# Seven block products in place of eight in 14 of the 44 weight pairs of a gated MLP's down product

## What is computed

```python
h = rms_norm(x, ln2[l])
u = h @ w_ffn_in[l]                        # 2048 -> 2 x 5632
a, b = jnp.split(u, 2, axis=-1)
a = causal_depthwise_conv(a, conv_w[l], conv_b[l])
x = x + (jax.nn.gelu(a, approximate=False) * b) @ w_ffn_out[l]   # 5632 -> 2048
return rms_norm(x, ln_f)
```

## Time and profile before

| | us |
|---|---|
| median of 3 runs | 1126.16 |
| lowest and highest | 1125.9, 1127.29 |
| the profiled execution's own time | 1127.33 |
| its span in the trace | 1125.5 |

### The profile page before, as it was taken

One profiled execution on the slowest core, in us unless ns is written; L12 is line 12 of the kernel. 1 busy time (PEld: TensorE's weight loads), 2 busy tenths in 40 slices (PEclk: granted clock), 3 DMA queues, 4 the chain that ended last, 5 costly groups with the idle time before them and its releaser, 6 DMA issues.

```text
span 1125.5 us, 16771 instructions
## 1 busy us (share of the span) xinstructions
PE 1105.9 (98%) x5746; PEld 936.6 (83%) x5746; DVE 693.5 (62%) x994; ACT 565.3 (50%) x800; POOL 75.2 (7%) x86
## 2 busy tenths in 40 slices
PE   7999999999999999999999999999999999999996
PEld 6888888877888888888888888888888788888885
DVE  4656666666655575665656656657566655575555
ACT  5545555555545454544544545445445444455443
POOL 2000111111100000101101101001011000000001
PEclk8999999999999999999999999999999999999999
DMA  9766555554566666666666666666665555556641
GB/s 338 246 188 174 155 165 149 162 155 150 161 190 177 182 187 188 188 187 186 188 190 187 189 190 189 188 187 186 186 187 189 196 191 193 195 186 200 197 133 75
DMA packets 146241, 206.80 MB, mean 184 GB/s; under 512 B 7540, under 2 KB 75538, under 8 KB 145953
## 3 DMA queue, kind: packets, MB, share of 16 engines
q1 hardware_dynamic: 145632, 204.67, 60.3%
q0 software_dynamic: 544, 1.72, 0.4%
q10 hardware_dynamic: 32, 0.01, 0.0%
HBM read 204.17 MB, written 2.10 MB: 183 GB/s over the span
## 4 chain that ended last, share of the span: by engine, by line
PE 97%; DVE 1%; DMA 1%; ACT 0%; SPq 0%; issue 0%; DVEq 0%; ACTq 0%
PE acc L634 14%; PE acc L414 13%; PE acc L416 13%; PE acc L415 13%; PE acc L640 7%; PE bank_s L634 7%; PE bank_tr L634 7%; PE bank_tr L640 4%; PE bank_s L640 4%; PE bank_s L416 2%; PE bank_s L414 2%; PE bank_s L415 2%; PE bank_tr L416 2%; PE bank_tr L414 2%; PE bank_tr L415 2%; DMA raw<-in_w_in 1%
## 5 line engine op out<-in xcount | busy, mean ns | idle before, releaser
L979 DVE TENSOR_TENSOR w_lo<-raw,w_hi 128x1024 fp32r<-128x1024 f32 x380 | 465.8, 1226 | 399.3 <-ACT w_hi L728 397.3
L728 ACT ACTIVATE w_hi<-raw 128x1024 fp32r<-128x1024 f32 x380 | 403.0, 1061 | 542.6 <-PE acc L416 168.0
L634 PE MATMUL acc<-h_both,w_hi 128*128 128x512 f32 x704 | 220.3, 394 | 0.0
L640 PE MATMUL acc<-h_both,w_lo 128*128 128x256 f32 x704 | 140.6, 282 | 0.0
L414 PE MATMUL acc<-w_hi,h_both 128*128 128x512 f32 (+1 forms) x352 | 139.4, 396 | 0.9 <-DVE h_both L986 0.9
L416 PE MATMUL acc<-w_hi,h_both 128*128 128x512 f32 (+1 forms) x352 | 134.6, 382 | 0.0
L415 PE MATMUL acc<-w_lo,h_both 128*128 128x512 f32 (+1 forms) x352 | 134.4, 382 | 0.0
L634 PEld LDWEIGHTS acc<-h_both,w_hi 128*128 128x128 f32 x704 | 121.1, 190 | 15.1
L640 PEld LDWEIGHTS acc<-h_both,w_lo 128*128 128x128 f32 x704 | 121.0, 190 | 13.7
L634 PE MATMUL bank_s<-h_both,w_hi 128*128 128x512 f32 x352 | 109.0, 391 | 0.0
L634 PE MATMUL bank_tr<-h_both,w_hi 128*128 128x512 f32 x352 | 109.0, 390 | 0.0
(11 more groups left out here) (168 smaller groups left out, 1340.1 us busy)
## 6 DMA issues: line engine op xcount, KB each, us to landing
raw<-in_w_ffn_in SPq DMA_DIRECT2D x176, 512.0 KB, 3.6
raw<-in_w_ffn_out SPq DMA_DIRECT2D x88, 512.0 KB, 4.7
raw<-in_w_in SPq DMA_DIRECT2D x128, 256.0 KB, 3.1
raw<-in_w_out SPq DMA_DIRECT2D x32, 512.0 KB, 4.0
raw<-in_w_in SPq DMA_DIRECT2D x20, 512.0 KB, 8.7
x_res<-in_x SPq DMA_DIRECT2D x4, 512.0 KB, 10.3
decay<-table_decay POOLq DMA_DIRECT2D x1, 1024.0 KB, 9.8
lnf_row<-in_ln_f SPq DMA_DIRECT2D x1, 1024.0 KB, 6.7
```

Source lines behind the costliest of these rows:

```text
L634: mm(out, w_hi[:, slot, q * COLS + ft * P:q * COLS + (ft + 1) * P], h_both[:, 2 * k + q, :, :].rearrange("p a n -> p (a n)"), start=k == 0 ...
L640: ins = mm(out, w_lo[:, slot, q * COLS + ft * P:q * COLS + (ft + 1) * P], h_hi[:, 2 * k + q, :], start=False, stop=k == 7 and q == 1, skip ...
L728: run(w_hi[:, n % SPLIT, :], raw[:, n % RAW, :], ACT.Copy).then_inc(hi_ready, 1)
L979: tt(w_lo[:, n % SPLIT, :], raw[:, n % RAW, :], w_hi[:, n % SPLIT, :].bitcast(F32), ALU.subtract).then_inc(lo_ready, 1)
```

## The change

**Seven products.** In 7 of the 22 pairs of each sweep (pairs 2, 5, 7, 10, 12, 15 and 17) the eight block products of a pair become seven, by Strassen's scheme in its form with few sums. Three of the seven take sums of weight blocks (`t_sum`, split to `t_hi` and `t_lo`), four take sums of activation blocks (`g_sums`). DVE makes four sums of 128x512 per such pair (`weight_sums`), one of them in place in the raw tile, so that ACT's rounding of the pair waits for the second sum. The results go to the sweep's own banks and to the four banks of the other sweep; `others_out` adds the latter to `x_res` with six DVE operations, once in a sweep, after a copy by ACT. `g_sums` is made once, in the last up group, by eight DVE operations.

**Pairs.** Weights are split two tiles at a time: one ACT operation and one DVE operation of 2048 columns, in a ring of 3 pairs instead of 4 tiles. There is one `t_sum`, one `t_hi` and one `t_lo`: `t_hi` of a pair waits until TensorE has finished the seven-product pair before it.

**First pairs.** `g_round` and `g_rest` of pairs 0 and 1 move into the last up group. The loops of the down product are written out; the load of `lnf_row` and four `times_gain` move later in the second sweep, the squares of the first sweep to after pair 24's split.

The diff, cut to what is spoken of:

```diff
-G_RING = 8
+PAIR_RING = 3
+DOWN_PAIRS = FFT // 2
+LAST_PAIR = 2 * DOWN_PAIRS - 1
+S_FIRST, S_STEP, S_COUNTS = (2, 5), 5, (4, 3)
+S_SLOT = {first + S_STEP * i: sum(S_COUNTS[:w]) + i
+          for w, (first, count) in enumerate(zip(S_FIRST, S_COUNTS)) for i in range(count)}
+S_PAIRS = sorted(S_SLOT)
+S_SUMS = 4 * len(S_COUNTS)
+X_ADDS = 6
+X_OUT_AT = 20
+GAIN_AT = 18
...
+                if m == 2 * (DOWN_PAIRS + 14) + 1:
+                    sp.wait_ge(g_lo_ready, DOWN_PAIRS + 12)
+                    sp.dma_start(lnf_row[:], ln_f.partition_broadcast(P)).then_inc(lnf_landed, 16)
...
+            def eight_products(r, banks, first=False, last=False):
+                pe.wait_ge(g_lo_ready, r + 1)
+                for half in range(2):
+                    pe.wait_ge(lo_ready, DOWN_TILE + 2 * r + (half + 1 if r < 2 else 2))
+                    for t in range(TOK):
+                        for c in range(2):
+                            ins = down_part(r, half, t, c, banks, first and half == 0, last and half == 1)
+                    ins.then_inc(tile_used, 1)
+            def seven_products(r, banks, others, first, last):
+                hi_g, lo_g, hi_b, lo_b = part_hi(r), part_lo(r), pair_hi(r), pair_lo(r)
+                left, right = slice(0, COLS), slice(COLS, 2 * COLS)
+                def product(out, block, rhs_hi, rhs_lo, starts, stops):
+                    return three_pass(out, hi_g[:, block, :], lo_g[:, block, :], rhs_hi, rhs_lo, starts, stops)
+                pe.wait_ge(g_lo_ready, r + 1)
+                pe.wait_ge(lo_ready, DOWN_TILE + 2 * r + 2)
+                product(others[0][:, 0, :], 0, hi_b[:, 0, left], lo_b[:, 0, left], first, last)
+                product(banks[0][:, 0, :], 2, hi_b[:, 1, left], lo_b[:, 1, left], False, False)
+                product(banks[1][:, 0, :], 7, hi_b[:, 1, right], lo_b[:, 1, right], False, False)
+                product(others[0][:, 1, :], 4, hi_b[:, 0, right], lo_b[:, 0, right], first, last)
+                pe.wait_ge(t_lo_ready, sevens_before(r) + 1)
+                product(others[1][:, 1, :], 6, t_hi[:, 0, :], t_lo[:, 0, :], first, last)
+                product(others[1][:, 0, :], 5, t_hi[:, 1, :], t_lo[:, 1, :], first, last)
+                product(banks[0][:, 1, :], 3, t_hi[:, 2, :], t_lo[:, 2, :], False, False).then_inc(tile_used, 2)
+            def down_pair(r, banks, others):
+                p = r % DOWN_PAIRS
+                if is_seven(r):
+                    seven_products(r, banks, others, p == S_PAIRS[0], p == S_PAIRS[-1])
+                else:
+                    eight_products(r, banks, p == 0, p == DOWN_PAIRS - 1)
...
+            for r in range(DOWN_PAIRS):
+                if r == S_PAIRS[0]:
+                    pe.wait_ge(b_sum_ready, GROUPS * 2)
+                down_pair(r, a_banks, b_banks)
+            pe.wait_ge(x_added, X_ADDS)
+            for r in range(DOWN_PAIRS, LAST_PAIR - 1):
+                if r == DOWN_PAIRS + S_PAIRS[0]:
+                    pe.wait_ge(ffn_added, 2 * TOK)
+                down_pair(r, b_banks, a_banks)
...
-                    pe.wait_ge(lo_ready, DOWN_TILE + m + 1)
+                    pe.wait_ge(lo_ready, DOWN_TILE + 2 * (m // 2) + 2)
                     pe.wait_ge(g_lo_ready, m // 2 + 1)
-                ins = down_part(0, c, (DOWN_TILE + m) % SPLIT, m % G_RING, b_banks, False, m == 87)
+                ins = down_part(m // 2, m % 2, 0, c, b_banks, False, m == 87)
...
+            def g_round(r):
+                if r >= PAIR_RING:
+                    act.wait_ge(tile_used, DOWN_TILE + 2 * (r - PAIR_RING + 1))
+                ins = run(part_hi(r)[:, 0:4, :], g_pair(r), ACT.Copy)
+                if is_seven(r):
+                    act.wait_ge(g_sums_ready, S_SUMS)
+                    ins = run(part_hi(r)[:, 4:8, :], g_sums[:, S_SLOT[r % DOWN_PAIRS]], ACT.Copy)
+                ins.then_inc(g_hi_ready, 1)
+            def hi_pair(r):
+                for n in (DOWN_TILE + 2 * r, DOWN_TILE + 2 * r + 1):
+                    act.wait_ge(raw_landed[n % RAW], landed_value(n))
+                act.wait_ge(tile_used, DOWN_TILE + 2 * max(0, r - PAIR_RING + 1))
+                k = sevens_before(r)
+                if is_seven(r):
+                    act.wait_ge(t_sum_ready, 4 * k + 2)
+                run(pair_hi(r), pair_raw(r), ACT.Copy).then_inc(hi_ready, 2)
+                if is_seven(r):
+                    if k:
+                        before = max(p for p in range(r) if is_seven(p))
+                        act.wait_ge(tile_used, DOWN_TILE + 2 * (before + 1))
+                    act.wait_ge(t_sum_ready, 4 * k + 4)
+                    run(t_hi[:], t_sum[:], ACT.Copy).then_inc(t_hi_ready, 1)
...
+                    if last and k in (10, 11):
+                        g_round(k - 10)
...
-            up_group(GROUPS - 1, FFN_TILE + GROUP_TILES * (GROUPS - 1), 0)
-            for m in (0, 2):
-                g_round(m // 2, m, m)
+            up_group(GROUPS - 1, FFN_TILE + GROUP_TILES * (GROUPS - 1), 0, True)
             b_copies(GROUPS - 1, DOWN_TILE)
...
-            def down_step(m, turn=0, first_kt=0):
-                if m % 2 == 0:
-                    g_round(turn * 4 + (m // 2 + 2), turn * 8 + first_kt, m + 4)
-                hi(DOWN_TILE + m + SPLIT, turn, 8, 16)
...
+            for r in range(2, LAST_PAIR + 1):
+                g_round(r)
+                hi_pair(r)
+                if r % DOWN_PAIRS == X_OUT_AT:
+                    others = (b_banks, a_banks)[r // DOWN_PAIRS]
+                    act.wait_ge(tile_used, DOWN_TILE + 2 * (r - X_OUT_AT + S_PAIRS[-1] + 1))
+                    run(u_sum[:], others[0][:, 0, :], ACT.Copy).then_inc(u_ready, 1)
+                if r == DOWN_PAIRS + 2:
                     for t in range(2 * TOK):
                         last_square_sum(t // TOK, t % TOK, t)
...
+            def g_rest(r):
+                dve.wait_ge(g_hi_ready, r + 1)
+                ins = tt(part_lo(r)[:, 0:4, :], g_pair(r), part_hi(r)[:, 0:4, :].bitcast(F32), ALU.subtract)
+                if is_seven(r):
+                    ins = tt(part_lo(r)[:, 4:8, :], g_sums[:, S_SLOT[r % DOWN_PAIRS]],
+                             part_hi(r)[:, 4:8, :].bitcast(F32), ALU.subtract)
+                ins.then_inc(g_lo_ready, 1)
+            def token_sums(w, k):
...
+                out, in0, in1, op = ((s1, g21, g22, ALU.add), (s3, g11, g21, ALU.subtract),
+                                     (s2, s1, g11, ALU.subtract), (s4, g12, s2, ALU.subtract))[k]
+                tt(out, in0, in1, op).then_inc(g_sums_ready, 1)
...
+                    if last and 3 <= k < 7:
+                        for w in range(len(S_COUNTS)):
+                            token_sums(w, k - 3)
+                    if last and k in (12, 13):
+                        g_rest(k - 12)
...
+            def weight_sums(r):
+                k = sevens_before(r)
+                both = pair_raw(r)
+                b11, b12 = both[:, 0, 0:COLS], both[:, 0, COLS:2 * COLS]
+                b21, b22 = both[:, 1, 0:COLS], both[:, 1, COLS:2 * COLS]
+                for n in (DOWN_TILE + 2 * r, DOWN_TILE + 2 * r + 1):
+                    dve.wait_ge(raw_landed[n % RAW], landed_value(n))
+                if k:
+                    dve.wait_ge(t_lo_ready, k)
+                tt(t_sum[:, 0, :], b22, b12, ALU.subtract).then_inc(t_sum_ready, 1)
+                tt(b12, b12, b11, ALU.subtract).then_inc(t_sum_ready, 1)
+                dve.wait_ge(t_sum_ready, 4 * k + 2)
+                tt(t_sum[:, 1, :], b22, b12, ALU.subtract).then_inc(t_sum_ready, 1)
+                dve.wait_ge(t_sum_ready, 4 * k + 3)
+                tt(t_sum[:, 2, :], b21, t_sum[:, 1, :], ALU.subtract).then_inc(t_sum_ready, 1)
+            def lo_pair(r):
+                dve.wait_ge(hi_ready, DOWN_TILE + 2 * r + 2)
+                tt(pair_lo(r), pair_raw(r), pair_hi(r).bitcast(F32), ALU.subtract).then_inc(lo_ready, 2)
+                if is_seven(r):
+                    dve.wait_ge(t_hi_ready, sevens_before(r) + 1)
+                    tt(t_lo[:], t_sum[:], t_hi[:].bitcast(F32), ALU.subtract).then_inc(t_lo_ready, 1)
...
+            def others_out(sweep):
+                others = (b_banks, a_banks)[sweep]
+                x_0, x_1, x_2, x_3 = others[0][:, 0, :], others[0][:, 1, :], others[1][:, 0, :], others[1][:, 1, :]
+                c0, c1 = (slice((2 * sweep + c) * COLS, (2 * sweep + c + 1) * COLS) for c in range(2))
+                y11, y21, y_2 = x_res[:, 0, c0], x_res[:, 1, c0], x_res[:, :, c1]
+                y2_ = x_res[:, 1, 2 * sweep * COLS:2 * (sweep + 1) * COLS].rearrange("p (c n) -> p c n", c=2)
+                done = sweep * X_ADDS
...
+                dve.wait_ge(tile_used, DOWN_TILE + 2 * (sweep * DOWN_PAIRS + S_PAIRS[-1] + 1))
+                dve.wait_ge(u_ready, sweep + 1)
+                tt(u_sum[:], u_sum[:], x_2, ALU.add).then_inc(x_added, 1)
+                tt(y11, y11, x_0, ALU.add).then_inc(x_added, 1)
```

(25 more changed lines are left out.)

170 lines of the change are left out of this document (70 added, 100 removed).

## The result

The changed kernel takes **1114.51 us** (median of 4 runs, 1114.27 to 1115.29) against 1126.55 (4 runs, 1125.9 to 1127.29) for the kernel before: a ratio of 0.9896, 95% interval 0.988 to 0.9912. The forecast was 1115.8 us, with a range of 1112.5 to 1121.8. The profiled execution of the changed kernel took 1114.47 us, that of before 1127.3.

A forecast was written before the change was run, and what follows sets the result against it. The prediction took TensorE, busy for 98% of the span, to bound the kernel. Its terms -9.5 - 5.0 + 4.1 = -10.4 us, against the median of 1126.2, gave 1115.8 us, with a range of 1112.5 to 1121.8.

The forecast's parts named there:

- Fewer products: Down product: 14 pairs have 21 matmuls for 24, so 42 matmuls at 0.227 us fall away, -9.5 us.
- First pairs: Passage from up to down product: early rounding removes TensorE's 3.3 us wait and 1.7 us of lower clock, -5.0 us.
- VectorE's new load: Down product: VectorE needs 24.7 us per five pairs against TensorE's 25.8, so it keeps up with 4% to spare.
- Waits anew: TensorE waits 1.3 us at pair 2, 0.7 at pair 6, 1.5 at pair 43, plus 0.6 for hand-overs: +4.1 us.
- Costed at nothing: Splitting two tiles in one operation, the `lnf_row` load and what follows the last matmul: no added time.
- The clock drops at the new waits: Rival: three clock drops cost 5.1 us, 1120.9 us; chance 0.17 together with VectorE operations 5% dearer.
- VectorE becomes the bound: Rival: VectorE idles during roundings, losing 2.8 us in each of about six five-pair stretches, 16.8 us: 1132.6 us; chance 0.07.
- The start is late: Rival: a split of the first pairs waits behind the last up tiles, losing the 5.0 us: 1120.8 us; chance 0.05.
- the saving is not there: Rival: extra hand-overs take 0.68 us in each of 14 pairs and the start's gain goes: 1126 us; chance 0.03.
- VectorE is never late: Rival: leads hide the three new waits of TensorE: 1111.7 us, up to 1114; chance 0.08.

The follow-up runs named there:

- e1_eight_products: The changed kernel with eight products in all 44 pairs, without the sums and `others_out`, early rounding kept: 1121.73 us, ratio 0.9959 to the kernel before.
- e7_pairs_only: The changed kernel with eight products everywhere and pairs 0 and 1 rounded behind the last up group: 1125.81 us, ratio 0.9991 to the kernel before.
- e2_late_rounding: The changed kernel with rounding and rest of pairs 0 and 1 put back behind the last up group, seven products kept: 1118.21 us.
- e3_gains_last: The changed kernel with the four gains moved from behind pair 40's split to behind pair 43's: 1114.18 us.
- e8_others_last: The changed kernel with `others_out` of the second sweep moved behind pair 43's split: 1113.33 us.
- e4_one_more_op: The changed kernel with one more unused VectorE operation of 512 columns ahead of the split in each of pairs 2 to 43: 1126.97 us.

## Why the prediction was right

**Fewer products, -9.5.** Right: from e1_eight_products to the changed kernel the down product is 6.93 us shorter, and the waits that came with it are 2.5. From e7_pairs_only to e2_late_rounding it is 9.6 shorter, which gives 9.5 again once the wait at pair 43 and the difference in the clock are counted.

**First pairs, -5.0.** Right: e1_eight_products has 5.00. That it fits so closely is because term and measurement use the same trace of the kernel before; against e7_pairs_only, where the clock stood lower for longer, the early rounding brings 6.0. The step "a `w_lo` and a `g_lo` (1.23 + 0.68 = 1.9 us) fit in a tile of 2.8 us" was wrong in its size: the two take 2.85 us there, since `g_lo` stands still for GpSimd. Nothing was left of VectorE's idle time, and TensorE did not wait.

**VectorE's new load, 24.7 of 25.8 us.** A little too high. Groups of the changed kernel by shape (times, then busy us and mean ns):

```profile
L1414 DVE TENSOR_TENSOR w_lo<-raw,w_hi 128x2048 fp32r<-128x2048 f32 x28 | 64.1, 2288 | 4.3 <-ACT w_hi L981 4.2
L1417 DVE TENSOR_TENSOR t_lo<-t_sum,t_hi 128x1536 fp32r<-128x1536 f32 x14 | 24.6, 1754 | 4.2 <-ACT t_hi L987 4.2
```

The durations were forecast within 0.02 us (2.31 and 1.77). But the next one starts 0.08 us before the end, so that in the queue an operation costs 0.605 at 512 columns, 1.67 at 1536 and 2.20 at 2048, where I took 0.64, 1.7 and 2.3. Five pairs need 3 x 2.81 + 2 x 5.08 + 2 x 2.66 = 23.9 us. The prediction weighed a section of the Trainium skill (VectorE: DVE Perf Modes, The TRN2 errata), by which SBUF latency is exposed between instructions, and drew from it that each operation costs its full duration. That conclusion is not what the rows show for operations that wait for nothing. A fixed cost for each instruction they do show, as the section has it: the intervals grow by 1.04 ns a column, which leaves 0.07 us of the 0.605 at 512 columns. Only an operation that needs the result of the one before starts 0.04 after its end.

**Waits anew, +4.1.** Mechanism and places right, the sum too high by 1.6, and this is the whole error of the sum in the down product: 11.9 us shorter for a forecast of 10.4. Pair 2: forecast 1.3 + 0.2, measured 1.39. Pair 6: forecast 0.7 + 0.2, measured 0.07, which is VectorE's 0.8 us per five pairs. Pair 43: forecast 1.5 + 0.2, measured 1.08, mostly since `others_out` takes 5.3 us in the queue and not 5.7; e3_gains_last and e8_others_last show that the wait was `others_out`'s.

**Costed at nothing.** Right for the splits of two tiles (e7_pairs_only) and for the loads: no wait of TensorE for a transfer in the down product. The end stayed at 10.3 us.

**The rivals.** *The clock drops at the new waits*: it did not, in any wait of the down product up to 2.1 us. *VectorE becomes the bound*: not in this kernel, but e4_one_more_op puts its point on record. The prediction had it at 1.9 us more than its 24.7 per five pairs, which is 26.6; measured was break-even at 23.9 + 3.0 = 26.9. That is near by luck: with the rival's own six stretches the gain of 10.4 is used up at 1.7 us each, 27.5 of VectorE, and in e4_one_more_op half the loss came at pair 43 and from the clock, which the rival does not have. *The start is late*, *the saving is not there* and *VectorE is never late* fall by the traces.

The forecast of 1115.8 missed by 1.3 us: 1.6 of waits forecast and not met, and 0.4 the other way, by which the second median of the kernel before (1126.55) lies above the first. Medians are good to about 1 us only, so that these terms close so well is partly luck; what carries the account is the length of the down product.

## What to carry to other kernels

When one engine's work is cut by giving another more, work out the second engine's queue for one period of the pattern, with the interval from start to start and not the duration: here 23.9 us of 25.8 held, and 26.9 gave all of it back, half of that at a single place near the end. An average that fits is not enough. Walk the first steps, where no lead is there yet, and the last ones, where single jobs stand in the queue: 2.5 us were lost there, and two changes of order alone brought 1.9 of them back, while two more of the cheap pairs, with the same average, cost 3.5.
